# A gated ConvFFN in two phases by halves of the output channels, with the activations parked in DRAM

## The reference, cut to what matters

```python
def _convffn(h, rows, l, p):
    up = jnp.einsum('bld,df->blf', h, p['ffn_w_up'][l])       # 1024 -> 2 * 2816
    up = _dwconv3(up, p['ffn_conv_w'][l], rows)               # depthwise, width 3, zero at row edges
    gate, val = jnp.split(up, 2, axis=-1)
    return jnp.einsum('blf,fd->bld', jax.nn.silu(gate) * val, p['ffn_w_down'][l])   # 2816 -> 1024
...
    x = x + g2 * _convffn(h, rows, l, p)
...
    y = rmsnorm(x, final_norm_w)
```

## Time and profile before

| | |
|---|---|
| median of three runs | 946.06 us (944.06 to 949.16) |
| span of the profiled execution (first to last instruction) | 942.4 us |
| median of the runs less that span | 3.7 us |
| TensorE busy, of the span | 921.2 us (98%) |
| VectorE busy | 595.1 us (63%) |
| ScalarE busy | 385.0 us (41%) |
| first matmul of the FFN, end of its last | 472.9 us, 935.6 us |
| granted TensorE clock, mean | 0.996 of 2.4 GHz |

### The profile page before, as it was taken

The page is one execution under the profiler, slowest core; times in us unless marked ns, Lnnn a source line. Parts: engine busy times, 40 slices in busy tenths (PEclk is TensorE's granted clock), DMA queues, the critical chain, the costliest instruction groups (busy, mean ns, idle before and its releaser), DMA issues.

```text
span 942.4 us, 13901 instructions
## 1 busy us (share of the span) xinstructions
PE 921.2 (98%) x5602; PEld 822.5 (87%) x5602; DVE 595.1 (63%) x764; ACT 385.0 (41%) x649; POOL 26.9 (3%) x36
## 2 busy tenths in 40 slices
PE   8999999999999999999999999999999999999997
PEld 4479898898898889687889999889999988999985
DVE  5754666957858866898676655345555534555556
ACT  5754433333333323232655544213444521244443
POOL 2200000100000001001000000000000000000000
PEclk9999999999999999999999999999999999999999
DMA  9664323423422443309022322222212222122102
GB/s 304 219 223 154 116 87 135 122 87 118 157 94 91 135 161 87 128 7 262 0 90 67 97 84 68 89 90 67 70 67 90 68 89 78 57 80 79 45 1 112
DMA packets 34343, 98.32 MB, mean 104 GB/s; under 512 B 3767, under 2 KB 11959, under 8 KB 33640
## 3 DMA queue, kind: packets, MB, share of 16 engines
q1 hardware_dynamic: 30776, 86.37, 27.8%
q0 software_dynamic: 3040, 10.78, 4.2%
q10 hardware_dynamic: 464, 0.30, 0.1%
HBM read 94.27 MB, written 3.16 MB: 103 GB/s over the span
## 4 chain that ended last, share of the span: by engine, by line
PE 78%; DVE 14%; ACT 3%; DMA 2%; issue 2%; ACTq 0%; DVEq 0%; SPq 0%; POOLq 0%
PE ps L1593 22%; PE ps L1594 22%; PE ps L1595 22%; PE ps L1814 3%; PE ps L1613 2%; PE ps L1674 1%; DVE w_lo L1088 1%; DMA raw<-in_slots 1%; DVE o_hg L1320 1%; PE ps L1826 1%; PE ps L1951 1%; DMA part<-in_rates 1%; DVE KK L1280 1%; PE ps L1834 1%; DMA w<-in_hy_w 1%
## 5 line engine op out<-in xcount | busy, mean ns | idle before, releaser
L1593 PE MATMUL ps<-h_hi,w_hi 128*128 128x320 f32 x1152 | 360.6, 313 | 2.1 <-DVE w_lo L1088 1.4
L1595 PE MATMUL ps<-h_hi,w_lo 128*128 128x320 f32 x1152 | 355.9, 309 | 0.0
L1594 PE MATMUL ps<-h_lo,w_hi 128*128 128x320 f32 x1152 | 355.9, 309 | 0.0
L1593 PEld LDWEIGHTS ps<-h_hi,w_hi 128*128 128x128 f32 x1152 | 216.5, 188 | 3.2 <-issue 2.3
L1594 PEld LDWEIGHTS ps<-h_lo,w_hi 128*128 128x128 f32 x1152 | 216.5, 188 | 0.1
L1595 PEld LDWEIGHTS ps<-h_hi,w_lo 128*128 128x128 f32 x1152 | 216.3, 188 | 0.0
L1088 DVE TENSOR_TENSOR w_lo<-raw,w_hi 128x1024 fp32r<-128x1024 f32 x106 | 129.4, 1225 | 109.3 <-ACT w_hi L727 103.5
L727 ACT ACTIVATE w_hi<-raw 128x1024 fp32r<-128x1024 f32 x106 | 110.8, 1052 | 93.1 <-PE ps L1595 90.6
L1594 PE MATMUL ps<-w_lo,a_hi 128*128 128x512 f32 x220 | 85.6, 389 | 0.0
L1593 PE MATMUL ps<-w_hi,a_hi 128*128 128x512 f32 x220 | 85.6, 389 | 0.0
L1595 PE MATMUL ps<-w_hi,a_lo 128*128 128x512 f32 x220 | 85.6, 389 | 0.0
(11 more groups left out here) (279 smaller groups left out, 1033.8 us busy)
## 6 DMA issues: line engine op xcount, KB each, us to landing
raw<-in_slots SPq DMA_DIRECT2D x138, 512.0 KB, 3.7
raw<-in_slots SPq DMA_DIRECT2D x24, 256.0 KB, 5.8
xin<-in_x_sample SPq DMA_DIRECT2D x4, 512.0 KB, 11.8
grow<-gates POOLq DMA_DIRECT2D x2, 1024.0 KB, 12.6
x<-in_x_sample POOLq DMA_DIRECT2D x2, 1024.0 KB, 13.6
out_y_sample<-x SPq DMA_DIRECT2D x4, 512.0 KB, 3.1
ktab<-in_ktab POOLq DMA_DIRECT2D x1, 1024.0 KB, 8.8
lead_hi<-in_slots SPq DMA_DIRECT2D x4, 256.0 KB, 10.9
```

The lines of the kernel that those rows point to most:

```text
L1593: mm(out, lhs[0], rhs[0], start=first, stop=False)
L1594: mm(out, lhs[0], rhs[1], start=False, stop=False)
L1595: return mm(out, lhs[1], rhs[0], start=False, stop=last)
```

## The change

The FFN no longer works in rounds. Phase A goes through the pairs one by one and does at once the down product of an earlier pair for the lower 512 output channels, with the five accumulators kept in PSUM banks 0 to 4 throughout; the activation of each pair is also written to DRAM (`acts`) by POOL. Phase B reads the activations back and does the down product for the upper 512 channels. A new form of up projection with seven products for each pair (`fast_pair`) is in the code, with sums of quarters of `h` (`hq`, `make_t`, `round_t`, `split_t`: `t_hi`, `t_lo`) and of weights; but `PLAIN` holds all 22 pairs, so that no pair takes that form. What is run for each pair from the third on is `plain_pair`. The sums of `h` are still made. The convolution loses its padded buffer: `xf` holds the bare 640 tokens, the outer taps are added on 630 of them, and ScalarE mends the one place where the last sample row meets the prompt row.

```diff
-ROUNDS = [(0, 8), (8, 8), (16, 6)]
+ROUNDS = [(0, NF)]
...
+PLAIN = tuple(range(NF))
+HEAD_HALVES = [(u, 0) for u in range(HEAD_UNITS)] + [(1, 1), (0, 1), (3, 1), (2, 1)]
+HEAD_PAIRS = HEAD_UNITS // 2
+PAIRS_DOWN = NF // 2
+RESIDENT = 4
...
+    for t in range(HEAD_PAIRS, NF):
+        out += [("up", t, 0), ("up", t, 1)]
+        if t % 2 == 0:
+            out.append(("down", 0, (t - HEAD_PAIRS) // 2))
+    out.append(("down", 0, PAIRS_DOWN - 1))
+    return out + [("down", 1, m) for m in range(PAIRS_DOWN)]
...
+            first_b = PLACE["down", 1, 0]
+            fetch(5, first_b)
+            for m in range(PAIRS_DOWN):
+                fetch(first_b + m, first_b + m + 1)
+                for f in (2 * m, 2 * m + 1):
+                    eng.wait_ge(sem(f"spilled{f % 2}"), 16 * (f // 2 + 1))
+                    if f < 4:
+                        eng.wait_ge(sem("fconv"), 2 * (NF - 1 + f // 2))
+                    else:
+                        eng.wait_ge(sem("b_split"), f - 3)
+                    load(xf[:, f % 4 // 2, f % 2, :], acts[f], f"ld_a{f % 4}")
...
+            for t in range(NF):
+                eng.wait_ge(sem("act_ready"), t + 1)
+                load(acts[t], actf[:, t % 2, :], f"spilled{t % 2}")
...
+                link(A(out, x, ACT.Copy, scale=taps[1]))
+                A(out[:, at:at + 1], x[:, at - 1:at], ACT.Identity, scale=taps[0], bias=out[:, at:at + 1])
+                A(out[:, at - 1:at], x[:, at:at + 1], ACT.Identity, scale=taps[2], bias=out[:, at - 1:at]).then_inc(sem("middle_tap"), 1)
...
+            def pair_step(t):
+                banks = [bank for bank, _ in UP_BANKS[t]]
+                plain = t in PLAIN
+                ffn_hi(t, 2)
+                middle_tap(t - 1, 0)
+                if plain:
+                    take_half(half_count(t, 1), banks[0], t, 1, 0)
+                else:
+                    take_p1(t)
+                gate_silu(t - 1)
+                if plain:
+                    take_half(half_count(t, 2), banks[1], t, 1, 1)
+                round_act(t - 1)
+                if t + 1 < NF:
+                    ffn_hi(t + 1, 1)
+                if plain:
+                    middle_tap(t, 1)
+                    take_half(half_count(t, 3), banks[2], t, 0, 0)
+                else:
+                    take_c11(t)
+                if t + 1 == NF:
+                    ffn_hi("B", 0)
+                    ffn_hi("B", 1)
+                elif t + 1 not in PLAIN:
+                    ffn_hi(t + 1, 0)
+                if not plain:
+                    middle_tap(t, 1)
+                ffn_hi(t + 1, 3)
+                if plain:
+                    take_half(half_count(t, 4), banks[0], t, 0, 1)
...
+            take_head(2)
+            take_head(3)
+            take_head(4)
+            middle_tap(0, 1)
+            round_t(0)
+            take_head(5)
+            middle_tap(0, 0)
+            round_t(1)
+            take_head(6)
+            gate_silu(0)
+            round_t(2)
+            round_act(0)
+            middle_tap(1, 1)
+            round_t(3)
+            take_head(7)
+            ffn_hi(HEAD_PAIRS, 1)
+            if HEAD_PAIRS not in PLAIN:
+                ffn_hi(HEAD_PAIRS, 0)
+            ffn_hi(HEAD_PAIRS, 3)
+            for t in range(HEAD_PAIRS, NF):
+                pair_step(t)
+            middle_tap(NF - 1, 0)
+            round_again(0)
+            round_again(1)
+            gate_silu(NF - 1)
+            ffn_hi("B", 2)
+            round_act(NF - 1)
+            round_again(2)
+            round_again(3)
+            ffn_hi("B", 3)
+            round_again(4)
+            round_again(5)
+            round_again(6)
+            round_again(7)
...
+            def pair_step(t):
+                fast, next_fast = t not in PLAIN, t + 1 < NF and t + 1 not in PLAIN
+                if t > HEAD_PAIRS and t - 1 not in PLAIN:
+                    product_sum(t - 1, C12)
+                ffn_lo(t, 2)
+                outer_pair(t - 1, 0)
+                if fast:
+                    product_sum(t, U2)
+                gated(t - 1)
+                if fast:
+                    product_sum(t, WW)
+                if next_fast:
+                    weight_sums(t + 1, 0)
+                    weight_sums(t + 1, 1)
+                split_act(t - 1)
+                if fast:
+                    product_sum(t, C22)
+                if next_fast:
+                    weight_sums(t + 1, 2)
+                if t + 1 < NF:
+                    ffn_lo(t + 1, 1)
+                if fast:
+                    product_sum(t, C21)
+                if t + 1 == NF:
+                    ffn_lo("B", 0)
+                    ffn_lo("B", 1)
+                elif next_fast:
+                    ffn_lo(t + 1, 0)
+                outer_pair(t, 1)
+                ffn_lo(t + 1, 3)
...
+            make_t(0)
+            make_t(1)
+            outer_pair(0, 1)
+            make_t(2)
+            outer_pair(0, 0)
+            split_t(0)
+            make_t(3)
+            gated(0)
+            split_t(1)
+            split_act(0)
+            split_t(2)
+            outer_pair(1, 1)
+            split_t(3)
+            ffn_lo(HEAD_PAIRS, 1)
+            if HEAD_PAIRS not in PLAIN:
+                ffn_lo(HEAD_PAIRS, 0)
+            ffn_lo(HEAD_PAIRS, 3)
+            for t in range(HEAD_PAIRS, NF):
+                pair_step(t)
+            if NF - 1 not in PLAIN:
+                product_sum(NF - 1, C12)
+            outer_pair(NF - 1, 0)
+            split_again(0)
+            split_again(1)
+            gated(NF - 1)
+            ffn_lo("B", 2)
+            split_act(NF - 1)
+            split_again(2)
+            split_again(3)
+            eng.wait_ge(sem("ld_gate2"), 16)
+            for i in range(NT):
+                eng.wait_ge(sem("down_made"), i + 1)
+                add(i, 0, "down_taken", "down_added")
+            ffn_lo("B", 3)
+            for f in range(4, 8):
...
+            def plain_pair(t):
+                banks = [bank for bank, _ in UP_BANKS[t]]
+                for j, (gv, half) in enumerate(((1, 0), (1, 1), (0, 0), (0, 1))):
+                    if j == 3:
+                        down_step(t - HEAD_PAIRS)
+                    if half == 0:
+                        slot_ready(t, 1 if gv else 2)
+                    name, value = UP_BANKS[t][j][1] if j < 3 else ("half_free", half_count(t, 1))
+                    eng.wait_ge(sem(name), value)
+                    slot, bank, cols = 1 if gv else 2, banks[j % 3], (LEFT, RIGHT)[half]
+                    quarters(bank, slot, 0, (h_hi, h_lo), A_HALF, cols, last=False)
+                    quarters(bank, slot, HW, (h_hi, h_lo), B_HALF, cols, first=False).then_inc(sem("half_made"), 1)
...
+            down_step(NF - 2)
+            down_again(0, range(3))
+            down_step(NF - 1)
+            down_again(0, range(3, NT)).then_inc(sem("b_done"), 1)
+            for m in range(1, PAIRS_DOWN - RESIDENT):
+                down_again(m, range(NT)).then_inc(sem("b_done"), 1)
+            steps = [(m, i) for m in range(PAIRS_DOWN - RESIDENT, PAIRS_DOWN) for i in range(NT)]
+            steps.sort(key=lambda step: (step[1] // 2, step[1] < 2 and step[0] == PAIRS_DOWN - 1, step[1]))
+            for m, i in steps:
+                done = down_again(m, (i,))
```

More of the change, by code:

```diff
@@ L482, in unit_free, with slot_free @@
             eng.wait_ge(sem(name), value)
+        def slot_free(eng, t, slot):
+            if t == "B":
+                if slot == 0:
+                    last = max(f for f in range(NF) if f not in PLAIN) if len(PLAIN) < NF else None
+                    name, value = ("head", 0) if last is None else ("prod_made", product_count(last, P2))
+                elif slot <= 2:
+                    name, value = free_after(NF, slot)
+                elif slot == 3:
+                    name, value = "down_made", NT
+                else:
+                    name, value = "b_done", slot - 3
+            else:
+                name, value = free_after(t, slot)
+            if name == "head":
+                name, value = "half_made", head_count(value, 1)
+            eng.wait_ge(sem(name), value)
@@ new lines, in free_after @@
+        def free_after(t, slot):
+            if slot == 3:
+                return ("head", 3) if t == HEAD_PAIRS else ("down_step", t - HEAD_PAIRS)
+            if slot == 0:
+                before = [f for f in range(t) if f not in PLAIN]
+                return ("prod_made", product_count(before[-1], P2)) if before else ("head", 0)
+            if t == HEAD_PAIRS:
+                return "head", slot
+            if t - 1 in PLAIN:
+                return "half_made", half_count(t - 1, 2 if slot == 1 else 4)
+            return "prod_made", product_count(t - 1, P7 if slot == 1 else P3)
@@ new lines, in _ @@
+            ffn_hi(HEAD_PAIRS, 3)
[14 more added lines that the diff above has]
+            round_again(7)
+            for m in range(4, PAIRS_DOWN):
```

(46 more changed lines are left out.)

435 lines of the change are left out of this document (282 added, 153 removed).

## The result

The changed kernel takes 965.18 us (median of 4 runs, 963.55 to 970.91), the kernel before in the same comparison 945.3 (944.06 to 949.16): a ratio of 1.0217, 95% interval 1.0193 to 1.0241. The profiled execution has a span of 961.7 us against 942.4. 962 was forecast, with a range of 952 to 972.

What follows compares the result with a forecast made beforehand. The prediction took the FFN to be bound by TensorE's matmuls. Span 942.4 + 9.5 (head) + 2.0 (clock) + 4.5 (change of phase) - 0.2 (end) = 958.2 us, plus 3.7 around it: 962, range 952 to 972.

Steps and rivals of the forecast that it cites:

- The basis, that only new waits count: In the FFN, TensorE has no idle time and matmuls stay the same, so only places where it comes to wait matter.
- The steady pair: Each of 20 pairs takes TensorE 17.5 us, other engines half idle, smallest slack 4.2 us, so nothing is lost.
- (b): A wait in every steady pair, from late gate weights or a blocked ScalarE queue: 20 x 1 us, 982; chance 0.06.
- (c): Phase B bound by its loads, a step taking 10.7 us: about 9 x 3.9 us, 997; chance 0.04.
- (d): Matmuls of 320 columns become denser, up to 13.3 ns each: 28 us gained, 934; chance 0.04.
- The head: Ninth half product waits for pair 2's value-weight split, queued behind the sums of h: 9.5 us lost, bounds 3.0 and 12.
- The clock at the head: After the stop at the head the clock falls and matmuls run at half pace: 2 us lost, bounds 0 and 3.5.
- The change of phase: From phase A to B, stalls of 1.8 and 2.4 us plus 0.2: 4.5 us lost, bounds 3 and 8, no clock loss.
- rival (a): Clock falls at both head and change of phase, up to 3.5 us more, or loads late, 4: 970; chance 0.17.
- T: End of pair 21's last half product; B2 expected landed about T + 8.7, bounds T + 7.3 and T + 11.
- The end: After the last matmul VectorE is free sooner for the last tile's add: -0.2 us at most.
- What lies around the span: 3.7 us added to the forecast span of 958.2 us to reach 962.

Runs made afterwards that it cites:

- e8: Changed kernel plus three or six extra ScalarE copies before each steady pair's gate-weight split: ratio 1.0234 with three; with six, one run, FFN 542.7 us.
- e3: Changed kernel with only the split of pair 2's value weights moved ahead of the sums of h: ratio 1.0163, FFN 477.8 us.
- e11: Changed kernel with seven-product pairs except 0 to 3 and 21, reordered change of phase, early value-weight split, most sums-of-h work moved later: ratio 0.9835.
- e7: Changed kernel with 60 extra matmuls of 320 columns, result thrown away, in the gap behind the eighth half product: ratio 1.0213.
- e1: Changed kernel without the sums of h that no product uses: ratio 1.018, FFN 480.8 us.
- e2: Changed kernel without the sums of h and with the split of pair 2's value weights moved ahead: ratio 1.0111, FFN 473.3 us.
- e4: Changed kernel with activations 0 and 1 split earlier and pair 21's activation work ahead of the split of B2: ratio 1.0194, FFN 481.9 us.

## Why the prediction was right

**The basis, that only new waits count: right.** The steady pair was 17.50 us for 17.5, without idle time; the slack 4.2 us, confirmed by e8. Rivals (b), waits in every pair, and (c), phase B bound by its loads, did not occur; nor (d), denser matmuls: the starts stay 0.147 us apart.

**The head: right in place, cause and size.** 9.57 us for 9.5; the fifth half product to the ninth took 23.7 us (489.12 to 512.85) for the 23.5 worked out. VectorE's chain of ten took 14.2 us for 14.3. That it is mostly a matter of order is shown by e3, where 3.9 us of gap are left with the same work, and by e11, where 1.8 are.

**The clock at the head: right.** 2.3 us for 2, shown apart by e7. The Trainium skill, TensorE: Matmul & The Clock Gate, section "The HAM clock gate", has throttled as the default and activity as what releases it; this trace agrees, with 4.65 us at 1.2 GHz after the gap.

**The change of phase: the mechanism right, one term wrong and one agreement by luck.** The gaps were 2.3 and 2.3 us for 1.8 and 2.4. But "I take no loss of clock here" failed: 3.4 us were lost, which is the clock's part of rival (a). The FFN is 20.5 us longer where the terms for the head, its clock and the change of phase add up to 16.0, and this one makes 3.4 of the 4.5 us that are missing. In the span 0.9 us of it doesn't show, because the FFN of the changed kernel happened to begin 0.9 us earlier (472.03 for 472.97), which no term had.

The second gap agrees by luck. B2 was taken to have landed at T + 8.7. T was 865.0, and ScalarE began to round B2 at 875.81, T + 10.8, just within the bound of T + 11; from the issue of B2 it took 5.8 us. TensorE didn't feel those 2.1 us, since it had itself lost 0.5 us more than forecast in the first gap and 1.7 us to the clock. Had the clock not fallen in between, the gap would have been 4.0 us; in e3, where it didn't fall there, it is 4.15 by starts. A wait that ends at a fixed time swallows what is lost ahead of it. The two gaps and the falls after them are 8.0 us in the changed kernel, and 8.2 in e3, with one fall and the longer gap. The end of the wait isn't fixed from run to run, though: B2 landed 5.8 us after its issue in the changed kernel, 6.0 in e3, 6.8 in e1 and 7.0 in e2. With 1.0 us more of gap and 1.2 more of slow matmuls, e1 kept only 2.0 of the 4 us that it had gained at the head.

**The end:** -0.2 us forecast; from the last start to the end of the span 7.13 us before and 6.95 after.

**What lies around the span:** 3.7 us were added to reach a median. Against the plain runs' median it is 3.5 for the changed kernel; the run with a span of 961.7 itself took 963.55, so 1.9 of it lies around the span and the rest is that this profile, like the one of before, was among the shortest runs.

So 962 for the median lies 3.2 us under the measured 965.2, and 958.2 for the span 3.5 us under 961.7; nearly all of both is the missing term.

**What stays open:** why B2 needs 5.8 us to land, and 5.2 to 7.2 over the other runs. The trace of the changed kernel rules one suspect out. POOL issues the last write to DRAM and the load of `fnw` at 871.98 and 872.51, but between 869.0 and 875.8 only SP's queue, q1, moves packets (packets, MB, share of the 16 DMA engines); those of POOL's queue begin at 876.95, after B2 has landed:

```profile
q1 hardware_dynamic: 571, 1.52, 72.7%
```

The two activations ahead of B2 and B2 itself are 1.18 MB, so some 0.34 MB of the loads issued right behind it (activations 4 and 5 and B3, from 870.54 on) went with them. Whether these delay B2 no run shows, since none moved them.

## What to carry to other kernels

Where TensorE has no idle time, a change of order can only lose, and what it loses can be read ahead by walking each engine's queue from the last instruction whose time does not change: the 9.5 us at the head could be added up from a few rows of durations. When a stall is taken away, walk the queues again with the earlier times: what was free in time only thanks to the stall is the next one, as the bank was in e4. Work that nobody reads is cheap on an idle engine and dear in front of a split that TensorE waits for.
